# A scan over chunks regrouped by pairs of directions, and a group norm's root on 16 rows

## The reference

```
def step(s, inp):
    r_t, k_t, v_t, kk_t, a_t, w_t = inp
    sa = jnp.einsum("dbhij,dbhj->dbhi", s, kk_t)
    s = (s * w_t[..., None, :] - sa[..., :, None] * (kk_t * a_t)[..., None, :]
         + v_t[..., :, None] * k_t[..., None, :])
    y = jnp.einsum("dbhij,dbhj->dbhi", s, r_t) if readout else None
    return s, y

kd = k[:, :, None] * (1 + (a - 1) * k_a)            # keys of each direction
yn = ((y - mu) * lax.rsqrt(var + GN_EPS)) * gn_g + gn_b   # mean and variance over each head
out = (yn + bonus) * gate
```

## Time and profile before

| | us |
|---|---|
| median of three runs | 1370.82 |
| the profiled execution | 1375.32 |
| its span, first to last instruction | 1373.5 |
| mean granted clock of PE | 0.969 of 2.4 GHz |

### The profile page before, as it was taken

The page is one execution under the profiler, slowest core; times in us unless marked ns, Lnnn a source line. Parts: engine busy times, 40 slices in busy tenths (PEclk is TensorE's granted clock), DMA queues, the critical chain, the costliest instruction groups (busy, mean ns, idle before and its releaser), DMA issues.

```text
span 1373.5 us, 25936 instructions
## 1 busy us (share of the span) xinstructions
PE 1286.6 (94%) x11356; PEld 949.4 (69%) x11356; DVE 543.0 (40%) x1188; ACT 339.9 (25%) x868; POOL 136.7 (10%) x207
## 2 busy tenths in 40 slices
PE   6999998999987899999989999999999959999996
PEld 2435888899976788888878887656677744445433
DVE  1256234343434599992040641674252150111113
ACT  2434243333221222110011211455431112101101
POOL 0002254455200000120000000000000010000000
PEclk9999999999998999999999999999999959999998
DMA  9600002221126243434343333211022376999992
GB/s 395 282 0 32 2 33 67 93 95 65 65 93 248 99 175 131 177 107 171 123 150 127 120 124 141 102 62 62 17 109 85 131 336 252 420 427 430 427 427 96
DMA packets 18544, 223.08 MB, mean 162 GB/s; under 512 B 2112, under 2 KB 3264, under 8 KB 3968
## 3 DMA queue, kind: packets, MB, share of 16 engines
q1 hardware_dynamic: 18032, 220.05, 41.0%
q0 software_dynamic: 256, 1.06, 0.3%
q10 hardware_dynamic: 144, 0.31, 0.1%
HBM read 220.37 MB, written 1.05 MB: 161 GB/s over the span
## 4 chain that ended last, share of the span: by engine, by line
PE 91%; DVE 3%; DMA 2%; ACT 2%; issue 1%; SPq 0%; ACTq 0%; DVEq 0%
PE ps L597 37%; PE ps L718 13%; PE ps L1135 8%; PE ps L945 6%; PE ps L1004 5%; PE ps L1179 4%; PE ps L1146 2%; PE ps L1050 2%; DMA mem<-weights 2%; PE ps L1116 2%; PE ps L1021 2%; PE ps L696 1%; PE ps L792 1%; PE ps L1035 1%; ACT mem L1444 1%
## 5 line engine op out<-in xcount | busy, mean ns | idle before, releaser
L597 PE MATMUL ps<-mem 128*128 128x256 f32 (+2 forms) x2096 | 521.5, 406 | 19.6 <-DVE mem L1745 8.3
L597 PEld LDWEIGHTS ps<-mem 128*128 128x128 f32 x2096 | 399.3, 192 | 130.9 <-issue 50.5
L718 PE MATMUL ps<-mem 64*64 64x64 f32 (+1 forms) x5664 | 185.5, 223 | 4.0 <-issue 4.0
L718 PEld LDWEIGHTS ps<-mem 64*64 64x64 f32 x5664 | 178.6, 137 | 14.6 <-issue 14.2
L1774 DVE SCALAR_TENSOR_TENSOR mem<-ps,mem 128x189 f32<-128x189 f32 (+2 forms) x352 | 148.3, 431 | 14.8 <-ACT mem L1390 3.9
L1135 PE MATMUL ps<-mem 128*64 128x512 f32 x512 | 111.6, 592 | 0.5 <-ACT mem L1511 0.5
L1135 PEld LDWEIGHTS ps<-mem 128*64 128x64 f32 x512 | 37.3, 137 | 72.9 <-issue 72.2
L1999 DVE TENSOR_TENSOR mem<-ps,mem 128x512 f32<-128x512 f32 x8 | 5.5, 693 | 187.3 <-PE ps L1135 187.3
L945 PE MATMUL ps<-mem 128*128 128x256 f32 x352 | 77.0, 378 | 0.0
L945 PEld LDWEIGHTS ps<-mem 128*128 128x128 f32 x352 | 66.5, 189 | 9.7
L1242 ACT ACTIVATE mem<-ps 128x256 f32<-128x256 f32 x128 | 49.2, 384 | 83.0 <-PE ps L718 80.4
(11 more groups left out here) (252 smaller groups left out, 1235.0 us busy)
## 6 DMA issues: line engine op xcount, KB each, us to landing
mem<-experts SPq DMA_DIRECT2D x48, 2048.0 KB, 17.4
mem<-weights SPq DMA_DIRECT2D x44, 2048.0 KB, 7.8
mem<-late_ada SPq DMA_DIRECT2D x16, 1024.0 KB, 5.1
mem<-weights SPq DMA_DIRECT2D x3, 1536.0 KB, 6.6
mem<-tokens SPq DMA_DIRECT2D x1, 2048.0 KB, 12.3
mem<-consts SPq DMA_DIRECT2D x1, 1504.0 KB, 23.5
out<-mem SPq DMA_DIRECT2D x1, 1024.0 KB, 4.8
mem<-consts POOLq DMA_DIRECT2D x1, 776.0 KB, 5.4
```

Of the source, the lines that this page charges most:

```text
L597: last = mm(bank(j % banks)[:, 0:nn], w[:, kc, c * P:(c + 1) * P], rr(kc), start=kc == 0, stop=kc == KD - 1)
L718: last = mm(out[hp, j], lhs[hp, j], rhs[hp, j], start=i == 0, stop=i == len(terms) - 1)
```

## The change

The scan is written anew, with jobs that cover both directions at once. `over_banks` lets one copy take both directions' results out of two neighbouring banks (512 columns, 1024 for the wide ones). In `heads` direction 0 goes low to low and high to high as before, and direction 1 goes low rows to high columns and high rows to low columns (`crossed`), except for `turned` and X3. A job is 32 matmul instructions.

The algebra of the chain is another one. Preparation makes removalsT, removals, A2, A2T, A4, Q1, W8, M, MT, turned, M2, M2T, M4T, and from step 4 keys_turned and X0; removalsT and M are 128 columns wide until step 3. Three products, X1, X2, X3 (128 columns wide from step 4), solve for all keys of the step with no state in it; two jobs `spread_solution`, one a direction, of 64 rows to 128 columns, combine them with the grams; then `state` is one product of 128 rows by 64 columns for each head and direction (32 instructions in all) that takes the values and the last state stacked on 128 partitions (VS), and `read_out` is another. What only the last product needs from the step before is the state, so fading and adding it go away; ACT and DVE copy it (`state0`, `state1`). Values are placed in VS by four transfers a step that SP issues behind the late piece's (`place_values`).

Of the keys kd and a times kk are made once for all tokens: ACT makes the factors (8 activations of 512 columns at projection chunk 9), POOL twelve products of 512 columns, DVE four; `stage_keys` is then three instructions a direction. `put_eyes` copies identities into the keys' places. POOL's other work is four sums with the identity and one mask a step, each for both directions. The Fourier mix over tokens is split in halves over passes 1 to 4, and the Fourier norm is made in pass 5, at the end of DVE's list of that pass. Each pass has its jobs in another order, shown below.

In the group norm the variances of the 8 heads and two token halves are summed into 16 rows of 128 columns (`head_rows`), rooted by one ACT instruction and inverted by one DVE instruction on 16x128, and spread over the partitions again by 16 matmul instructions with 16 rows (`one_head`, an identity widened by a DVE copy of 16x1024), from whose PSUM bank the scaling reads. The terms of the bonus need three DVE steps less.

```diff
--- before.py
+++ after.py
...
+            def place_values(s):
+
+                if s == 0:
+                    sp.wait_ge(S("proj"), 19)
+                    sp.wait_ge(S("values_kept"), 4)
+                elif s == 1:
+                    sp.wait_ge(S("keys_staged"), EARLY_KEYS)
+                else:
+                    sp.wait_ge(*turn("state_made", s - 2))
+                    if s - 2 >= READ_FROM:
+                        sp.wait_ge(*each_reading("y_made", s - 2))
+                for d in range(2):
+                    for hp, rows in ((0, LOW), (1, HIGH)):
+                        sp.dma_start(VS[s % 2][VALUES[d], d, hp, :, :], VT[chunk_at(s, d) // C][rows, :, :])\
+                            .then_inc(S("values_placed%d" % (s % 2)), 16)
...
+            def heads(b, width, lhs, rhs, crossed=True):
+
+                out = over_banks(b, width)
                 for j in range(NJ):
-                    for i, (lhs, rhs) in enumerate(terms):
-                        for hp in (slice(0, 64), slice(64, 128)):
-                            last = mm(out[hp, j], lhs[hp, j], rhs[hp, j], start=i == 0, stop=i == len(terms) - 1)
+                    for hp in (LOW, HIGH):
+                        mm(out[hp, 0, j], lhs[hp, 0, j], rhs[hp, 0, j], start=True, stop=True)
+                    for hp, to in ((LOW, HIGH), (HIGH, LOW)) if crossed else ((LOW, LOW), (HIGH, HIGH)):
+                        last = mm(out[to, 1, j], lhs[hp, 1, j], rhs[hp, 1, j], start=True, stop=True)
                 return last
 
-            def made(name, last):
-                last.then_inc(turns_of(name), 1)
-
-            def grams(s):
+            def product(name, b, lhs, rhs, width=C, crossed=True):
+
+                heads(b, width, lhs, rhs, crossed).then_inc(turns_of(name), 1)
...
+            def turned(s):
+                if s >= READ_FROM:
+                    waits(s, "M_kept")
+                    product("X0", prep_bank(s, 0), W8, WR[:, :, :, C:3 * C], 2 * C)
+                waits(s, "MT_kept")
+                product("turned", prep_bank(s, 1), RX[s % 2][:, :, :, FIRST], KX[s % 2][:, :, :, C:3 * C], 2 * C,
+                        crossed=False)
...
+            def spread_solution(s, d):
+
+                if d == 0:
+                    waits(s, "X3_kept", "reads_kept", "gram_kept")
+                else:
+                    waits(s, "for_state0", "for_values0")
+                width = C if s < READ_FROM else 2 * C
+                for j in range(NJ):
+                    o = [bank(CHAIN + hp)[:, j * width:(j + 1) * width] for hp in range(2)]
+                    for hp, rows in ((0, LOW), (1, HIGH)):
+                        mm(o[hp], KX[s % 2][rows, d, j, C:3 * C], RX[s % 2][rows, d, j, C:C + width],
+                           start=True, stop=False)
+                    for hp, rows in ((0, LOW), (1, HIGH)):
+                        last = mm(o[hp], GR[rows, j, 2 * d:2 * d + 2, :].rearrange("p a c -> p (a c)"),
+                                  XB[rows, d, j, 0:width], start=False, stop=True)
+                last.then_inc(turns_of("spread%d" % d), 1)
+
+            def state(s):
+                waits(s, "for_state0", "for_state1", "for_values0", "for_values1")
+                if s == 0:
+                    pe.wait_ge(S("state_cleared"), 2)
+                else:
+                    waits(s - 1, "state0", "state1")
+                if s < NJ:
+                    pe.wait_ge(S("mixed_kept"), s + 1)
+                elif s == NJ:
+                    pe.wait_ge(*norm_root("four"))
+                pe.wait_ge(S("values_placed%d" % (s % 2)), 64 * (s // 2 + 1))
+                for r in range(2):
+                    for j in range(NJ):
+                        for d in range(2):
+                            at = (r * NJ + j) * C
+                            last = mm(bank(SIDE)[STATE[d], at:at + C], KF[:, d, r, j, FIRST], VS[s % 2][:, d, r, j, :],
+                                      start=True, stop=True)
+                last.then_inc(turns_of("state_made"), 1)
...
             for i in range(1, STEPS + 1):
-                late_piece(i - 1, 0)
                 if i < STEPS:
-                    grams(i)
-                held(i - 1)
+                    removals(i)
+                if i >= 2:
+                    turn_piece(i - 2, 1)
+                if i < STEPS:
+                    other_removals(i)
+                first_factor(i - 1)
                 if i < STEPS:
                     squares_of_near(i)
-                if i == 1:
-                    waits(0, 1, "R3_kept")
-                    norm_sums("four", squares_f, NJ, TX, 6)
-                halfway(i - 1)
+                second_factor(i - 1)
+                if i <= NJ:
+                    token_spectrum(i - 1, 0)
+                else:
+                    late_piece(i - 1, 0)
                 if i < STEPS:
                     fourths_of_near(i)
-                else:
-                    turn_piece(i - 1, 0)
-                    late_piece(i - 1, 1)
-                removed(i - 1)
+                third_factor(i - 1)
                 if i < STEPS:
+                    part_of_near(i)
+                    turned_keys(i)
+                if i <= NJ:
+                    late_piece(i - 1, 0)
+                elif i < STEPS:
                     inverse_of_near(i)
-                    turn_piece(i - 1, 0)
-                    state(i - 1)
-                if i >= 5:
-                    if i == 5:
-                        pe.wait_ge(*norm_root("four"))
-                    read_out(i - 1)
+                spread_solution(i - 1, 0)
+                if i <= NJ:
+                    inverse_of_near(i)
+                    token_spectrum(i - 1, 1)
+                elif i == NJ + 1:
+                    waits(i - 2, "state0", "state1")
+                    norm_sums("four", squares_f, NJ, TX, SIDE)
                 if i < STEPS:
                     far_part(i)
-                    late_piece(i - 1, 1)
+                spread_solution(i - 1, 1)
+                turn_piece(i - 1, 0)
+                if i < STEPS:
+                    turned(i)
+                    state(i - 1)
                     squares_of_far(i)
+                if i - 1 >= READ_FROM:
+                    read_out(i - 1)
+                late_piece(i - 1, 1)
+                if i < STEPS:
                     fourths_of_far(i)
-                turn_piece(i - 1, 1)
-                if i < STEPS:
-                    inverse_of_far(i)
+            turn_piece(STEPS - 1, 1)
...
+                for half in range(2):
+                    m = NJ * half + j
+                    last = mm(bank(6)[0:16, 0:P], cst("head_rows")[:, 14 - 2 * m:30 - 2 * m],
+                              ysq[:, j, half * P:(half + 1) * P], start=m == 0, stop=m == 2 * NJ - 1)
+            last.then_inc(S("mix_sums"), 1)
+            pe.wait_ge(S("y_sum"), 3)
+            pe.wait_ge(S("y_centred"), NJ)
+            for j in range(NJ):
+                for half in range(2):
+                    m, at = NJ * half + j, (j % 2) * TX + half * P
+                    last = mm(bank(2 + j // 2)[:, at:at + P],
+                              one_head[:, 2 * m:2 * m + 2, :].rearrange("p a c -> p (a c)"),
+                              y[0:16, 1, 1, 0:P], start=True, stop=True)
+                last.then_inc(S("mix_sums"), 1)
             pe.wait_ge(S("y_scaled"), NJ)
...
+            act.wait_ge(*mix_sums("var", 1))
+            A(y[0:16, 1, 0, 0:P], bank(6)[0:16, 0:P], ACT.Sqrt, scale=1.0 / HEAD, bias=GN_EPS).then_inc(S("var_root"), 1)
...
+            dve.wait_ge(S("var_root"), 1)
+            V_.reciprocal(y[0:16, 1, 1, 0:P], y[0:16, 1, 0, 0:P]).then_inc(S("y_sum"), 1)
...
+            def raise_one(s, name, dst, src, ready):
+                pool.wait_ge(*turn(ready, s))
+                tt(dst, src, eye, ALU.add).then_inc(turns_of(name), 1)
+
+            pool.wait_ge(S("proj"), 11)
+            put_eyes(0)
             stage_keys(0)
             pool.wait_ge(S("proj"), 15)
             for i in range(STEPS):
+                raise_one(i, "Q0_kept", Q, B1, "A_kept")
+                pool.wait_ge(*turn("removalsT_copied", i))
+                tt(WR[:, :, :, FIRST], AO, far, ALU.mult).then_inc(turns_of("far_kept"), 1)
+                pool.wait_ge(*turn("far_kept", i))
+                raise_one(i, "A2_raised", A2I, B3, "A2_kept")
+                if 1 <= i < STEPS - 1:
+                    stage_keys(i + 1)
+                raise_one(i, "MT_raised", MTI, B1, "MT_kept")
```

More of the change, by code:

```diff
@@ L295, in two_blocks @@
         ms = Places(mem, ring_at, ring_at + RING * WBLK)
-        def both(*shape):
-            return [ms.take(*shape) for _ in range(2)]
-        KB1, RO1, GK1 = both(NJ, 2, C), both(NJ, 2, C), both(NJ, 2, C)
-        GU = [both(NJ, C) for _ in range(2)]
-        assert ms.at == ring_at + WBLK
-        EX, EI = both(NJ, C + 1), both(NJ, C)
+        pair = (2, NJ, C)
+        pairs = (2, NJ, 2 * C)
+        triples = (2, NJ, 3 * C)
```

(68 more changed lines are left out.)

718 lines of the change are left out of this document (383 added, 335 removed).

## The result

The changed kernel takes **1354.8 us** (median of four, 1354.7 to 1358.7) where the kernel before took 1371.7 beside it: ratio 0.9883, 95% interval 0.9863 to 0.9904. It is faster by 16.9 us; I had forecast 36.3. The profiled execution is the slowest of the four, 1358.7; that of the kernel before lay 4.5 above its median too, so the two tables of stretches can be set side by side.

A forecast was written before the change was run, and what follows sets the result against it. PE's own instructions were taken to bound the scan. From 135.4 us, 240.0 against 273.6, less 1.3 and 2.0 taken back, gave -30.3; norm and output product -6.0; together -36.3 from 1370.8: 1334.5 us, range 1314 to 1360.

The forecast's parts named there:

- PE bounds, the others hide: In the scan, PE's own instructions set the time and the other engines hide; only pass 8 and norm are chain-bound.
- The rate: Crossed narrow 64x64 products on PE: 23 ns an instruction, 0.74 us a job, between bounds of 14.6 and 29.5 ns.
- rival (1): Crossed jobs use four quarters fully, 14.6 ns; 8 of 27 us return as copy waits; 1316 us, chance 0.20.
- Stalls that wait for nothing: PE stalls within a job that wait for nothing the trace shows: 2.0 us taken back.
- SP's new placements: Four DMAs a step behind a 1 MB late piece: cost nothing unless the placement lands over 10 us late.
- The clock: At the output product's cold start, a shorter idle ahead of it gains 1.8 us.
- Keys of step 0: POOL's key products, ahead of removals of step 0, end at 138 or 141 us; 1.3 us taken back.
- Passes: Waits priced in passes: 2.2 us for reads of step 1, 2.9 for the Fourier norm, 0.8 at A2.
- Pass 8: Last pass, no step beside it, so all hops show: 20.0 us against 16.8, a loss of 3.2.
- Norm: Group norm chain with shorter root and reciprocal: 11.3 us against 15.5, a gain of 4.2.
- (4): Hops between stages each 0.45 us longer than the rows say add about 22 us; with (2) 1357 to 1374; chance 0.12.
- (2): PE's stream is limited by starts at 29.5 ns, so narrow jobs gain nothing: +17, 1351 us; chance 0.24.

The follow-up runs named there:

- after: The changed kernel as described, all parts of the change against the kernel before; 1354.8 us, ratio 0.9883.

## Why the prediction was wrong

**PE bounds, the others hide.** Right for before and still so after: crossed or not makes 35 us of difference.

**The rate.** I took 23 ns between bounds of 14.6 and 29.5. It is 14.6, rival (1)'s., which I read as "possible in a burst", was the row to go by. The Trainium skill ("TensorE: Matmul & The Clock Gate", Part 1) puts starts no closer than about 25 ns; after's rows have pairs at 29 ns and four starts in 58, so across four quarters it doesn't hold here, for a stream either. But the gain per pass was only 1.0 us (22.1 of work for 23.1), not the 3.5 of thirteen jobs: a narrow job that follows another shape holds PE for 0.63 us and a second one for 0.46 more, and with some ten such changes a pass the 0.45 us I had for all switches were 1.6. X3 of the first four steps, which isn't crossed, took 0.88 where my thirteen jobs had it at 0.74. Spreads took 1.93 us for 1.83, state and read-out 1.08 for 0.94, the turned product 1.89 for 1.75, each 0.10 to 0.14 us above its price.

**Stalls that wait for nothing.** The step that failed. I saw one of 1.59 us in the earlier trace rows, allowed 2.0 for all, and named fetching as what could eat the gain without pricing it. It was 13.8. With the load cut away 17.7 of the 20.3 us between forecast and result go, 1.8 of them the wait for its data: these stalls and the clock behind them are what the sum lacked. The row had its cause beside it: before loads the same 1 MB a piece, and its 1.59 us stall stands at the same place of a packet's 256 instructions as those of after, behind 1.05 MB of data. At half the rate it met one such stall of that length, not five. Besides, I judged SP's new placements by when their data was needed (a whole pass later: right) and not by what else uses the DMA engines at that moment. "They cost nothing" was wrong by about half of the gaps, 7 us in the run with the placements cut down.

**The clock.** The forecast had 1.8 us of gain from a warm clock at the output product and nothing for new cold stretches. They cost 13 us in the scan against 6 before, 7.4 of them in passes with a stall for instructions, the rest behind the waits for POOL and DVE and in pass 8. The output product gained 0.7, since the idle of 8.35 us of the earlier trace rows became 1.33 and 0.97 among short work and the granted clock is still 0.81 there.

**Keys of step 0.** The wait was 3.67 us for the 1.3 taken. I had POOL's products at 1.04, 1.25 at worst. They took 1.3 to 1.7:

```profile
123.83 1.27 POOL L2263 TENSOR_TENSOR mem<-mem 128x512 f32<-128x512 f32 x1
...
127.98 1.72 POOL L2264 TENSOR_TENSOR mem<-mem 128x512 f32<-128x512 f32 x1
```

and DVE's four beside them 1.54 each (6.17 us in all) where it takes 0.69 alone. The Trainium skill ("GPSIMD Engine Reference", 1. Specifications) says that the two contend when a VectorE instruction has two inputs in SBUF; these have, and the trace agrees.

**Passes.** Reads of step 1 2.9 for 2.2, Fourier norm 3.6 for 2.9, masks at A2 0.6 to 1.0 for 0.8: right in place and nearly in size. (The terms I gave for pass 5 add up to 27.7, not 27.9.) That the Fourier norm costs its wait was wrong: it covered a gap.

**Pass 8.** 23.0 for 20.0: all hops show as told (1.14, 1.12, 1.48, 1.01), the late data's 1.84 us and a cold start come on top.

**Norm.** 11.64 for 11.3: right. The spread's last scaling ends as forecast.

**Rivals.** (4), hops binding, would have given 1357 to 1374, near to what came, for the wrong reason: copies cost what I had. (2) gave 1351 with a rate that isn't so. (1) had the rate right and missed the time by 39 us, since it returned 8 us for copies and nothing for instructions and clock. The sum: from 133.36 to 417.20 us after takes 283.8, the forecast 262.7. Gaps 11.8 more, cold clock in the scan 13.0, output product 1.1, keys, reads and Fourier norm 3.8, together 29.7 where 21.1 are missing; the other -8.6 is PE's work below my price, 1.0 a pass, and what I can't split further. Not tried: whether another DMA order at the very start of the kernel matters, and what the clock alone costs, since no run changes it without changing the waits.

## What to carry to other kernels

When an engine's stream gets twice as fast, its supply of instructions must too: look at the instruction queue's packets beside every burst of data, and space the bursts by what the engine is doing, not by when the buffer falls free. A stall "for nothing" in the trace of before can be a price per burst, and here it grew with the rate: one of 1.59 us before, five of 2.0 to 3.6 after. Test removed waits together: on one chain a wait may be another shortage's cover, so that edits worth nothing alone (here 1.4 lost and 0.3 gained) can be worth 7 to 9 us beside the one that removes the shortage.

## What the runs showed of the hardware

Matmuls of 64x64 in four quarters run at 14.6 ns a start with a load for each (29.4 in two quarters), though pairs write the same bank. PE's instructions come in 16 KB packets of 256 (251 of them matmuls and loads), in after's passes 2 to 7 3.4 to 6.9 us apart where PE doesn't stall for them. Around a burst of 1 MB plus 256 KB two packets lay 5.5 to 7.7 us apart at the five stalls, and PE resumed 2.5 to 2.7 us after the second one's start. Two products on 512 columns, one on VectorE and one on GpSimd, slow each other from 0.69 to 1.54 and from 1.04 to 1.7 us.
